# Attention scores made one slot ahead, between the projection part and the value matmuls

## The chip, the cores and the metric

The kernel runs on one NeuronCore of a Trainium2 chip. TensorE (PE; its weight loads are shown as PEld), VectorE (DVE), ScalarE (ACT), GpSimd (POOL) and SyncE (SP) run their own instruction queues, each in order, and meet through semaphores. The metric is the device time of one execution in microseconds (us); the time before is the median of 3 runs, 701.91 us.

## What is computed

One layer, a gated stick-breaking attention, on x of 1024 tokens x 1024 features in float32, with a final RMSNorm:

```python
def stick_breaking_attention(q, k, v):          # 16 heads of 64, blocks of 128 queries
    ...
        mask = key_pos[None, :] < q_pos[:, None]
        z = jnp.einsum('bhqd,bhkd->bhqk', qb, kf) * scale
        log_beta = jax.nn.log_sigmoid(z)
        log_1m = jnp.where(mask, log_beta - z, 0.0)
        after = lax.cumsum(log_1m, axis=3, reverse=True) - log_1m
        a = jnp.where(mask, jnp.exp(log_beta + after), 0.0)
        return jnp.einsum('bhqk,bhkd->bhqd', a, vf)

h = rmsnorm(x, norm_g[0])
q, k, v, gate = jnp.split(h @ w_in, 4, axis=-1)
y = (attention(q, k, v) * silu(gate)) @ w_out
out = rmsnorm(x + y, final_g)
```

The kernel makes a = sigmoid(z) times a running product of sigmoid(-z) from the diagonal down; the running product is one scan on VectorE.

## The kernel before

Heads go in 8 pairs, and each pair has 16 slots; a slot s stands for query block i = s mod 8 of head s // 8 of the pair. Block i has 128 (i + 1) keys, so the work of a block grows through each half of a pair. Pairs 1 to 6 are a loop; pair 7 is written out; after it come the first slots of a tail (pair 8). Every engine runs the same list of slots in its own order, and only semaphores tie them together.

TensorE in slot s (`slot`, L600): the scores of block s (`scores`, L567; slots 0 and 8 make two blocks, slots 1 and 9 none), in slots 6 and 8 a transposition of the values of the next pair (`transpose_v`), 12 matmuls of the next pair's projection (`project_part`, L585; 6 in the first half of pair 7, and parts of the output projection after that), the value matmuls (L632) of the blocks of `a` that were transposed in the slot before, and the transposes (L644) of some blocks of `a`. The transposes of slots 4 to 7 take query blocks 0 to 3 of head 0, slots 8 to 11 blocks 4 to 7 of head 0, slots 12 to 15 blocks 0 to 3 of head 1, and slots 0 to 3 of the next pair blocks 4 to 7 of head 1. So the first transpose of slot 8 and that of the next pair's slot 0 wait (L642, `a_ready`) until the last and widest block, 7 or 15, is finished: "a boundary" in what follows.

ScalarE in slot s: it evacuates a finished projection half on even slots (L719, waits for `proj_done`), in slots 1, 5, 9 and 13 it moves a part of the output sums (L786, waits for the value matmuls of the slot before), then it copies the transposes of slot s-1 out of PSUM (L794; it waits for `t_done`), and only behind these it makes the two sigmoids of block s from the score bank z_ps[s mod 2] (L809 into `rest`, L811 into `a_group`; they wait for `z_ready`). VectorE in slot s: low parts of the splits, the gate product (L982, slots 0 and 14), the low part of the transposed blocks (L1000), and then the scan of block s (L1016). GpSimd in slot s: the product of sigmoid and scan (L1115), which gives `a_ready`, and in s mod 4 = 1 and 2 a weight split behind it (L1091).

The score matmuls wait for `beta_ready` (L576), so a score bank is written again only when the sigmoids of the block two before are done. The transposes and their copies have two banks.

Of the kernel before, what the change touches and what calls it, by code (L numbers as in the profile page):

```python
# [31 lines left out]
SLOTS = 16  # L32
# [41 lines left out]
def is_last(p):  # L74
    return isinstance(p, int) and p == PAIRS - 1


def is_tail(p):
    return isinstance(p, int) and p == PAIRS


def is_first(p):
    return isinstance(p, int) and p == 0


def wait(eng, sem, value):

    if not isinstance(value, int) or value > 0:
        eng.wait_ge(sem, value)
# [16 lines left out]
def v_t_at(p, s):  # L106
    return None if isinstance(p, int) and p >= PAIRS - 1 else STEADY[s][0]


def proj_slots(p):  # L110

    return range(SLOTS // 2) if is_last(p) else range(SLOTS)


def proj_part(p, s):

    if is_last(p):
        return s // 4, 2 * (s % 4), 2 * (s % 4) + 1
    return (s % 4) // 2, 4 * (s % 2), 4 * (s % 2) + 3
# [53 lines left out]
def z_offset(i):  # L173

    return 2 * P if P * (i + 1) == HALF + P else 0


def stick_breaking_layer(nc, x, norm_g, w_in, w_out, final_g, out):
# [3 lines left out]
    with ExitStack() as ctx:  # L182
# [41 lines left out]
        def q_of(par, hh):  # L224
            return arena[:, par, 0, hh * S:(hh + 1) * S]

        def k_of(par, hh, swapped):
            return arena[:, par, 2 if swapped else 1, hh * S:(hh + 1) * S]
# [4 lines left out]
        def w_out_of(half, hl):  # L233
            return arena[:, half, 2 * hl:2 * hl + 2, :].rearrange("p a (b n) -> p (a b) n", n=HALF)
# [70 lines left out]
        block = ctx.enter_context(nc.Block())  # L305
# [176 lines left out]
        def _(pe):  # L482
            def project(ring, bank, half, b):

                for n, (wl, hl) in enumerate(((0, 0), (0, 1), (1, 0))):
                    mm = nc.tensor.matmul(bank[:, :], w_split[:, ring, wl, b, :],  # L486
                                          hT[:, hl, b, half * HALF:(half + 1) * HALF],
                                          start=(b == 0 and n == 0), stop=(b == KB - 1 and n == 2))
                return mm
# [45 lines left out]
            def project_out(n, b):  # L535

                nh, tokens = n // KB, slice((n % KB) * P, (n % KB + 1) * P)
                at = ORDER.index(n)
                partial = n < PARTIAL_TILES and b < PAIRS - 1
                last = PAIRS - 2 if partial else KB - 1  # L540
                first = PAIRS - 1 if n < PARTIAL_TILES and not partial else 0
                if n == 0 and partial or n == ORDER[0] and b == KB - 1 or n == KB:
                    pe.wait_ge(wo_ready, n // KB * KB + b + 1)
                if n in (0, GQ) and b < PAIRS - 1:
                    pe.wait_ge(o_loaded[n // GQ][b], 32)
                if n == ORDER[0] and b == PAIRS - 1:
                    pe.wait_ge(o_lo, 2 * PAIRS)
                if b == first:


                    if n == 0 and partial:
                        pe.wait_ge(stage_ready, 2 * UNITS0 + 8 * (PAIRS - 1) + 2)
                    elif partial or at == 0:
                        pe.wait_ge(partial_sum, n)
                    elif at < BANKS:
                        pe.wait_ge(beta_ready, SLOTS * PAIRS)
                    else:
                        pe.wait_ge(y_sum, at - BANKS + 1)
                bank = proj_ps if partial else y_banks[at % BANKS]
                for m, (ol, wl) in enumerate(((0, 0), (0, 1), (1, 0))):  # L560
                    mm = nc.tensor.matmul(bank[:, :], hT[:, ol, b, tokens], w_out_of(nh, wl)[:, b, :],  # L561
                                          start=(b == first and m == 0), stop=(b == last and m == 2))
                if partial and b == last:
                    mm.then_inc(partial_done, 1)
                return mm

            def scores(p, par, s):  # L567

                hh, i = s // 8, s % 8
                width = P * (i + 1)  # L570
                if s == 0:
                    pe.wait_ge(qk_split, 4 * p + 4)
                    pe.wait_ge(k_swapped, 64 * p + 64)
                    if is_first(p):
                        pe.wait_ge(xt_lo, 2 * KB)
                wait(pe, beta_ready, SLOTS * p + s - 1)  # L576
                z, q, first = z_ps[s % 2], q_of(par, hh)[:, i * P:(i + 1) * P], z_offset(i)
                for c in range(0, first + width, HALF):
                    c0, c1 = max(c, first), min(c + HALF, first + max(width, 2 * P))
                    for swapped in (False, True):  # L580
                        mm = nc.tensor.matmul(z[:, c0:c1], q, k_of(par, hh, swapped)[:, c0 - first:c1 - first],  # L581
                                              start=not swapped, stop=swapped)
                mm.then_inc(z_ready, 1)

            def project_part(p, s):  # L585

                half, b0, b1 = proj_part(p, s)
                unit = 0 if is_last(p) else s // 4
                if half == 0:

                    pe.wait_ge(w_ready, 2 * UNITS0 + 8 * p + 2 * unit + b0 // 4 + 1)
                if b0 == 0:

                    pe.wait_ge(stage_ready, 2 * UNITS0 + 8 * p + 2 * unit + half - (is_first(p) and s == 0))
                for b in range(b0, b1 + 1):
                    mm = project((UNITS0 + unit) % 2, proj_ps, half, b)
                if b1 == KB - 1:
                    mm.then_inc(proj_done, 1)

            def slot(p, par, s):  # L600
                q_late = is_first(p) and s == 0
                if q_late:
                    project_part(p, s)
                if not is_tail(p):

                    for block in {0: (s, s + 1), 1: ()}.get(s % 8, (s,)):
                        scores(p, par, block)
                if v_t_at(p, s) is not None:
                    t = v_t_at(p, s)

                    transpose_v(t_base(p) + t, t % 2, 2 * UNITS0 + 8 * p + 2 + (s == 8), int(s == 8))
                if not is_tail(p) and s in proj_slots(p) and not q_late:
                    project_part(p, s)
                if isinstance(p, int):
                    for _ in range(EARLY_BY_SLOT.get((p, s), 0)):
                        project_out(*early.pop(0))

                for t, av, ahh, grp, j in av_at(p, s):
                    apar = 1 - par if s < 5 else par
                    pe.wait_ge(t_lo, t_base(p) + t + 1)  # L620
                    if j == 0:

                        group = {1: -1, 5: 0, 9: 1, 13: 2}[s]
                        wait(pe, o_summed, 4 * p + group)
                    rel = max(0, j - GQ * grp)
                    for hl in range(2):
                        if rel == GQ - 1:
                            c, moving = HALF - 2 * P, aT_pad[:, hl, :]
                        else:
                            c = rel * P  # L630
                            moving = aT[:, av % 2, hl, c:HALF]
                        mm = nc.tensor.matmul(o_ps[:, c:HALF], v_of(apar)[:, j, 2 * ahh:2 * ahh + 2, :]  # L632
                                              .rearrange("p x d -> p (x d)"), moving,
                                              start=(j == 0 and hl == 0),
                                              stop=(j == GQ * (grp + 1) - 1 and hl == 1))
                    mm.then_inc(av_done, 1)

                for t, av, thh, grp, j in units_at(p, s):
                    wait(pe, t_lo, t_base(p) + t - 1)
                    if j == 0:  # L640

                        pe.wait_ge(a_ready, SLOTS * p + (0 if s < 4 else 4 * (s // 4)))  # L642
                    for i2 in range(max(0, j - GQ * grp), GQ):
                        last = nc.tensor.transpose(t_ps[t % 2][:, i2 * P:(i2 + 1) * P],  # L644
                                                   a_g[grp][:, i2, j * P:(j + 1) * P], ident[:, :])
                    last.then_inc(t_done, 1)

            over_pairs(pe, slot, 4)


# [500 lines left out]
```

## Time and profile before

| | |
|---|---|
| median of 3 runs | 701.91 us (701.83 to 701.91) |
| profiled execution | 702.83 us, span 701.0 us |
| granted TensorE clock, mean | 0.992 |
| PE busy | 673.1 us (96%) |
| PEld busy | 565.2 us (81%) |
| DVE busy | 483.1 us (69%) |
| ACT busy | 426.4 us (61%) |
| POOL busy | 308.0 us (44%) |

A line of a timeline gives the start and the duration in us, the engine, the line of the kernel, the operation, what it writes and reads, how many instructions are merged in it, and in brackets how long its engine was idle ahead of it and what released it. Ends of matmuls are modelled: successive matmuls overlap in the records, so the pace of TensorE is read from the starts.

### The profile page before, as it was taken

Reading aid. Unit: us, or ns where it says so; the run is one execution under the profiler, and the core shown is the slowest. Engines: PE = TensorE matmul, PEld = TensorE weight load, DVE = VectorE, ACT = ScalarE, POOL = GpSimd, SP = SyncE. Lnnn points to the kernel's source line nnn. Section 1 sums busy time; section 2 is a strip of 40 time slices with the busy share of each in tenths; the row PEclk is TensorE's granted clock in tenths of the full one; section 3 lists DMA queues with packets and bytes.
Section 4 is the critical chain, followed back from the end, with each engine's and each line's share of the span. In section 5 each row is a group of like instructions: output and inputs, shape, how many; then the busy total and the mean of one; then the engine's idle time right before and its main releaser. Section 6 shows DMA issues by size and latency. Waiting matters only on the chain.

```text
span 701.0 us, 10872 instructions
## 1 busy us (share of the span) xinstructions
PE 673.1 (96%) x3426; PEld 565.2 (81%) x3426; DVE 483.1 (69%) x636; ACT 426.4 (61%) x795; POOL 308.0 (44%) x225
## 2 busy tenths in 40 slices
PE   5999999999999999999999999999999997999995
PEld 4787888888888888888888888888888776888884
DVE  5835657786678676867677667766776798735565
ACT  5614757676767676767676767666766674622322
POOL 2122544555464546454655464546363643315100
PEclk9999999999999999999999999999999998999998
DMA  7131310141114111510042014201421148522342
GB/s 284 46 95 41 94 43 16 63 119 32 31 57 124 31 32 37 135 39 22 23 135 60 15 31 120 75 15 30 120 60 30 60 136 295 201 91 90 121 146 95
DMA packets 28122, 57.64 MB, mean 82 GB/s; under 512 B 3376, under 2 KB 3376, under 8 KB 28080
## 3 DMA queue, kind: packets, MB, share of 16 engines
q1 hardware_dynamic: 25312, 51.13, 24.2%
q10 hardware_dynamic: 2736, 6.03, 2.3%
q8 instruction: 16, 0.26, 0.1%
q14 instruction: 26, 0.21, 0.1%
q0 software_dynamic: 32, 0.00, 0.0%
HBM read 37.23 MB, written 11.53 MB: 70 GB/s over the span
## 4 chain that ended last, share of the span: by engine, by line
PE 67%; DVE 12%; POOL 10%; issue 7%; ACT 3%; DMA 1%; POOLq 0%; DVEq 0%; ACTq 0%
PE proj_ps L486 31%; PE t_ps L644 8%; PE o_ps L632 8%; PE z_ps L561 8%; DVE rest L1016 7%; PE z_ps L581 5%; POOL a_group L1115 5%; POOL w_split L1091 5%; PE proj_ps L561 4%; PE o_ps L486 2%; DVE aT L1000 1%; DMA a_group<-x 1%; ACT stage L719 1%; ACT gate L776 1%; DVE gate L982 1%
## 5 line engine op out<-in xcount | busy, mean ns | idle before, releaser
L486 PE MATMUL proj_ps<-hT,w_split 128*128 128x512 f32 x1464 | 359.9, 394 | 2.1 <-DVE hT L889 1.4
L486 PEld LDWEIGHTS proj_ps<-hT,w_split 128*128 128x128 f32 x1464 | 269.9, 188 | 57.6 <-DVE hT L889 2.3
L1115 POOL TENSOR_TENSOR a_group<-a_group,rest 128x128 f32<-128x128 f32 (+7 forms) x128 | 160.6, 1257 | 279.2 <-DVE rest L1016 279.2
L1016 DVE TENSOR_TENSOR_SCAN rest<-rest,restart 128x128 f32<-128x128 f32 (+7 forms) x128 | 213.4, 1668 | 16.0 <-ACT rest L809 15.5
L1091 POOL TENSOR_TENSOR w_split<-w_raw,w_split 128x512 fp32r<-128x512 f32 x64 | 115.6, 1807 | 38.0 <-DVE w_split L851 38.0
L1000 DVE TENSOR_TENSOR aT<-t_ps,aT 128x512 fp32r<-128x512 f32 (+2 forms) x160 | 93.2, 607 | 40.1 <-ACT aT L794 38.8
L794 ACT ACTIVATE aT<-t_ps 128x512 fp32r<-128x512 f32 (+2 forms) x160 | 80.2, 532 | 65.8 <-PE t_ps L644 64.6
L581 PE MATMUL z_ps<-arena 128*128 128x512 f32 (+2 forms) x384 | 96.3, 366 | 0.3 <-DVE arena L938 0.3
L938 DVE TENSOR_TENSOR arena<-stage,arena 64x512 fp32r<-64x512 f32 x64 | 43.9, 686 | 69.4 <-ACT arena L739 68.8
L644 PE MATMUL t_ps<-ident,a_group 128*128 128x128 f32 x576 | 84.9, 275 | 4.7 <-POOL a_group L1115 4.4
L809 ACT ACTIVATE rest<-z_ps 128x128 f32<-128x128 f32 (+7 forms) x128 | 83.9, 655 | 8.9 <-PE z_ps L581 8.6
L632 PE MATMUL o_ps<-aT,arena 128*128 128x512 f32 (+2 forms) x320 | 82.9, 365 | 1.7 <-DVE aT L1000 1.7
L811 ACT ACTIVATE a_group<-z_ps 128x128 f32<-128x128 f32 (+7 forms) x128 | 84.3, 659 | 0.0
L644 PEld LDWEIGHTS t_ps<-ident,a_group 128*128 128x128 f32 x576 | 69.4, 142 | 15.1 <-issue 7.1
L719 ACT ACTIVATE stage<-proj_ps 128x512 f32<-128x512 f32 x61 | 36.5, 598 | 62.4 <-PE proj_ps L486 62.4
L632 PEld LDWEIGHTS o_ps<-aT,arena 128*128 128x128 f32 x320 | 60.0, 189 | 16.5 <-DVE aT L1000 3.7
L581 PEld LDWEIGHTS z_ps<-arena 128*128 128x128 f32 x384 | 59.6, 190 | 5.1 <-DVE arena L938 0.8
L561 PE MATMUL z_ps<-arena,hT 128*128 128x512 f32 x246 | 57.7, 391 | 0.0
L786 ACT ACTIVATE oT<-o_ps 64x512 f32<-64x512 f32 x32 | 19.0, 592 | 60.5 <-PE o_ps L632 60.5
L561 PEld LDWEIGHTS z_ps<-arena,hT 128*128 128x128 f32 x246 | 45.8, 188 | 9.4
L990 DVE TENSOR_TENSOR oT<-o_ps,oT 64x512 f32<-64x512 f32 x32 | 22.0, 689 | 24.9 <-ACT oT L786 24.8
L746 ACT ACTIVATE w_split<-w_raw 128x512 fp32r<-128x512 f32 x56 | 35.9, 641 | 0.5
(86 smaller groups left out, 454.2 us busy)
## 6 DMA issues: line engine op xcount, KB each, us to landing
w_raw<-w_in SPq DMA_DIRECT2D x64, 256.0 KB, 2.7
arena<-arena SPq DMA_DIRECT2D x32, 256.0 KB, 4.3
wo_raw<-w_out SPq DMA_DIRECT2D x16, 256.0 KB, 3.7
o_hi_scratch<-o_split SPq DMA_DIRECT2D x14, 256.0 KB, 2.1
o_lo_scratch<-o_split SPq DMA_DIRECT2D x14, 256.0 KB, 2.4
hT<-o_hi_scratch SPq DMA_DIRECT2D x14, 256.0 KB, 4.9
hT<-o_lo_scratch SPq DMA_DIRECT2D x14, 256.0 KB, 5.8
a_group<-x SPq DMA_DIRECT2D x14, 256.0 KB, 3.4
```

The source lines that it names most:

```text
L486: mm = nc.tensor.matmul(bank[:, :], w_split[:, ring, wl, b, :], hT[:, hl, b, half * HALF:(half + 1) * HALF], start=(b == 0 and n == 0), st ...
L561: mm = nc.tensor.matmul(bank[:, :], hT[:, ol, b, tokens], w_out_of(nh, wl)[:, b, :], start=(b == first and m == 0), stop=(b == last and m ...
L581: mm = nc.tensor.matmul(z[:, c0:c1], q, k_of(par, hh, swapped)[:, c0 - first:c1 - first], start=not swapped, stop=swapped)
L632: mm = nc.tensor.matmul(o_ps[:, c:HALF], v_of(apar)[:, j, 2 * ahh:2 * ahh + 2, :] .rearrange("p x d -> p (x d)"), moving, start=(j == 0 an ...
L644: last = nc.tensor.transpose(t_ps[t % 2][:, i2 * P:(i2 + 1) * P], a_g[grp][:, i2, j * P:(j + 1) * P], ident[:, :])
L794: nc.scalar.activation(to, t_ps[t % 2][:, rel * P:HALF], ACT.Copy).then_inc(t_hi, 1)
L809: nc.scalar.activation(rest[:, s % 2, S - width:S], z_ps[s % 2][:, first:first + width], ACT.Sigmoid, scale=-SCALE).then_inc(rest_ready, 1)
L811: nc.scalar.activation(a_g[grp][:, i % GQ, 0:width], z_ps[s % 2][:, first:first + width], ACT.Sigmoid, scale=SCALE).then_inc(beta_ready, 1)
L1000: nc.vector.tensor_tensor(lo, t_ps[t % 2][:, rel * P:HALF], hi.bitcast(F32), ALU.subtract).then_inc(t_lo, 1)
L1016: nc.vector.tensor_tensor_scan(span, span, restart[:, S - 1:(S - 1 - width if width < S else None):-1], 0.0, ALU.mult, ALU.max).then_inc(s ...
L1091: nc.gpsimd.tensor_tensor(to[:, 1], w_raw[:, part, :].rearrange("p (b n) -> p b n", b=4), to[:, 0].bitcast(F32), ALU.subtract).then_inc(w_ ...
L1115: nc.gpsimd.tensor_tensor(a, a, rest[:, s % 2, S + 1 - width:S + 1], ALU.mult).then_inc(a_ready, 1)
```

## The change

In a slot of TensorE the scores move from the front of the slot to behind the projection part (and behind the parts of the output projection), ahead of the value matmuls, and they are those of the next block. The last slot of a pair makes block 0 of the next pair. Each slot of a pair then makes one block of scores. The first slot of the first pair has the order that it had. Nothing is changed on the other engines, and no wait or count is changed.

```diff
             def slot(p, par, s):
-                q_late = is_first(p) and s == 0
-                if q_late:
-                    project_part(p, s)
-                if not is_tail(p):
-
-                    for block in {0: (s, s + 1), 1: ()}.get(s % 8, (s,)):
-                        scores(p, par, block)
                 if v_t_at(p, s) is not None:
                     t = v_t_at(p, s)
 
                     transpose_v(t_base(p) + t, t % 2, 2 * UNITS0 + 8 * p + 2 + (s == 8), int(s == 8))
-                if not is_tail(p) and s in proj_slots(p) and not q_late:
+                if not is_tail(p) and s in proj_slots(p):
                     project_part(p, s)
                 if isinstance(p, int):
                     for _ in range(EARLY_BY_SLOT.get((p, s), 0)):
                         project_out(*early.pop(0))
+
+                if is_first(p) and s == 0:
+                    scores(p, par, s)
+                if s < SLOTS - 1 and not is_tail(p):
+                    scores(p, par, s + 1)
+                elif not is_last(p) and not is_tail(p):
+                    scores(p + 1, 1 - par, 0)
 
                 for t, av, ahh, grp, j in av_at(p, s):
```

## Rows read from the trace of the kernel before

**Rows 1.** Waits, whole span: who waited for whom, us in total, times, longest.
```profile
ACT aT L794 <- PE t_ps L644: 64.6, 61, 3.5
...
ACT rest L809 <- PE z_ps L581: 8.6, 18, 0.7
...
PE t_ps L644 <- POOL a_group L1115: 4.4, 12, 1.2
```
**Rows 2.** Timeline of a steady pair's slots 13 to 15 and next slot 0.
```profile
323.99 0.59 ACT L786 ACTIVATE oT<-o_ps 64x512 f32<-64x512 f32 x1 [1.30 <-PE o_ps L632]
324.14 0.94 PE L581 MATMUL z_ps<-arena 128*128 128x512 f32 x4
...
327.87 1.55 POOL L1115 TENSOR_TENSOR a_group<-a_group,rest 128x768 f32<-128x768 f32 x1 [2.02 <-DVE rest L1016]
...
329.14 0.83 DVE L982 TENSOR_TENSOR gate<-stage,gate 128x512 f32<-128x512 f32 x1 [1.42 <-ACT gate L776]
...
329.37 1.75 POOL L1091 TENSOR_TENSOR w_split<-w_raw,w_split 128x512 fp32r<-128x512 f32 x1
...
330.41 2.59 DVE L1016 TENSOR_TENSOR_SCAN rest<-rest,restart 128x896 f32<-128x896 f32 x1
...
332.51 1.18 PE L581 MATMUL z_ps<-arena 128*128 128x512 f32 x4
332.87 0.38 ACT L794 ACTIVATE aT<-t_ps 128x256 fp32r<-128x256 f32 x1 [1.17 <-PE t_ps L644]
333.15 1.78 POOL L1115 TENSOR_TENSOR a_group<-a_group,rest 128x896 f32<-128x896 f32 x1 [2.03 <-DVE rest L1016]
...
333.53 2.90 PE L486 MATMUL proj_ps<-hT,w_split 128*128 128x512 f32 x12
333.73 1.03 ACT L809 ACTIVATE rest<-z_ps 128x1024 f32<-128x1024 f32 x1 [0.47 <-PE z_ps L581]
...
334.79 2.29 DVE L1016 TENSOR_TENSOR_SCAN rest<-rest,restart 128x1024 f32<-128x1024 f32 x1 [1.07 <-ACT rest L809]
334.88 3.29 POOL L1091 TENSOR_TENSOR w_split<-w_raw,w_split 128x512 fp32r<-128x512 f32 x1
...
336.27 0.40 PE L632 MATMUL o_ps<-aT,arena 128*128 128x256 f32 x2
...
337.85 0.86 DVE L982 TENSOR_TENSOR gate<-stage,gate 128x512 f32<-128x512 f32 x1 [0.77 <-ACT gate L776]
...
338.12 2.45 POOL L1115 TENSOR_TENSOR a_group<-a_group,rest 128x1024 f32<-128x1024 f32 x1
...
340.71 1.06 PE L644 MATMUL t_ps<-ident,a_group 128*128 128x128 f32 x8 [0.34 <-POOL a_group L1115]
```
**Rows 3.** Timeline of a steady pair's slot 7 and slot 8.
```profile
298.10 1.77 POOL L1115 TENSOR_TENSOR a_group<-a_group,rest 128x896 f32<-128x896 f32 x1 [2.02 <-DVE rest L1016]
...
299.23 2.79 DVE L1016 TENSOR_TENSOR_SCAN rest<-rest,restart 128x1024 f32<-128x1024 f32 x1 [0.36 <-ACT rest L809]
...
303.06 2.48 POOL L1115 TENSOR_TENSOR a_group<-a_group,rest 128x1024 f32<-128x1024 f32 x2
```
**Rows 4.** Timeline of the longest stall, in pair 7's slot 8.
```profile
585.26 0.79 PE L632 MATMUL o_ps<-aT_pad,arena 128*128 128x256 f32 x2 [4.16 <-DVE aT_pad L1000]
```
**Rows 5.** Windows (stretch, length, busy of each engine, PEclk, DMA share, GB/s).
```profile
553.70:555.00 1.30, 0.05 (x2) 0.05 (x1) 1.30 (x1) 0.59 (x1) 1.14 (x1) 1.00 0.87 274
585.30:590.00 4.70, 4.70 (x16) 4.22 (x17) 3.77 (x7) 3.37 (x7) 0.84 (x2) 0.50 0.92 285
568.00:586.00 18.00, 12.15 (x61) 9.42 (x61) 17.94 (x16) 11.25 (x20) 10.70 (x6) 0.95 0.54 178
```
**Rows 6.** Timeline of TensorE in a slot 9, which has no scores before.
```profile
306.15 3.02 PE L486 MATMUL proj_ps<-hT,w_split 128*128 128x512 f32 x12
...
309.00 1.10 PE L632 MATMUL o_ps<-aT,arena 128*128 128x512 f32 x4
```
**Rows 7.** Timeline: GpSimd's product of block 15 of pair 7, ahead of the tail.
```profile
614.71 2.00 POOL L1115 TENSOR_TENSOR a_group<-a_group,rest 128x1024 f32<-128x1024 f32 x1 [2.29 <-DVE rest L1016]
```

## The prediction, written before the changed kernel was run

> **What bounds the kernel now.** The busy times come first: TensorE is busy for 673.1 us of a span of 701.0, the others for 483 at most, so what is to be won or lost is in the 28 us in which it isn't, and part of those lies ahead of the first matmul and in the tail. Then the waits, all engines together [rows 1]. There the reader sees three things. ScalarE waits for transposes (L794) 61 times, 64.6 us in all. It waits for scores (L809) only 18 times, 8.6 us. And TensorE itself waits for GpSimd's product (L1115) at the transposes 12 times, 4.4 us. A timeline shows which these are: the boundaries, where the first transpose of slot 8 or slot 0 needs block 7 or 15. There are 15 that the product can end (slot 8 of pairs 0 to 6, slot 0 of pairs 1 to 7, and the tail's slot 0), and TensorE stands at nearly all of them, for 0.2 to 0.35 us in a steady pair. So a steady pair is bound by TensorE, but the chain that ends in `a_ready` arrives at each boundary with no slack. What makes this chain later makes the kernel longer by as much.
>
> The chain at a slot-0 boundary [rows 2]: the transposes of slot 14 leave ScalarE's copy at 332.87; the sigmoid of block 15 starts at 333.73 after 0.47 us of waiting for its scores; the scan starts at 334.79 and ends at 337.08; GpSimd's weight split, 3.29 us long, ends at 338.17; the product of block 15 ends at 340.57; TensorE goes on at 340.71, 0.34 late. One more stall stands by itself, 4.16 us in slot 8 of pair 7 [rows 4], where VectorE is the bound: it is busy for 17.94 of 18.00 us before it [rows 5].
>
> My sums are made against the profiled execution, 702.83 us (span 701.0 and 1.8 around it). The median is 0.92 lower, and I take that off at the end.
>
> **What is the same.** The same matmuls, transposes and waits are issued; no DMA, no instruction of another engine, nothing of SP's queue moves. At the end of a projection part both orders have done the same work, and at the end of slots 0 and 8 as well. So `proj_done` and the boundary's own transposes keep their place if nothing stalls. The scores were made before the projection part of their slot and are now made a slot ahead, so the wait of 0.47 us at L809 goes. I give it nothing: the sigmoid of block s is queued on ScalarE behind the copy of slot s-1's transposes, so early scores lie unused in their bank.
>
> **What becomes late: the transposes.** In slot s the value matmuls and transposes now stand behind the scores of s+1. For the same work done, they end later by the time of these scores. Slot 14: the scores of block 15 start at 332.51 and the projection at 333.53, 1.02 us [rows 2]. The copy at L794 moves from 332.87 to 333.89. It is 0.38 long and the sigmoid can start some 0.26 after its start, at 334.15 in place of 333.73: 0.42 later. Before, the copy lay beside the scores; now it lies behind them. This is the floor of the cost, 0.42 us a boundary.
>
> **It begins two slots earlier and grows in the queues.** In slot 13 the value matmuls are later by the scores of block 13 (0.78: start at 324.14, projection at 324.92), and ScalarE's L786 already waits for them there, 1.30 us [rows 2]. So sigmoid, scan and product of block 13 move by 0.78: the product from 327.87 to 328.65, its end to 330.2. The gate product L982 at 329.1 to 329.4 then meets it. VectorE's operations on two SBUF operands and GpSimd's go one after the other in this trace: the scan at 299.23 takes 2.79 where another of the same shape takes 2.29, and the product of block 6 ends 0.64 after its start [rows 2, 3]; the weight split at 334.88 is 3.29 long, and 1.09 of it is left when the scan ends [rows 2]. By that: L982 runs to 330.8, the weight split to 331.95, the scan of block 14 to 333.85 (before 333.0), the product of block 14 to 335.75 (before 334.93). The scan of block 15 could start at 335.2 but runs from 335.75 to 338.0 (before 337.08), the weight split to 339.1, L982 (0.65) to 339.75 and the product, 2.00 long by itself [rows 7], to 341.75 with a little handing over, where it was 340.57. That is 1.15 us a slot-0 boundary.
>
> The same steps at slot 8 [rows 3]: the product of block 6 ends at about 300.4 (before 299.87), for the scan of block 5 is held back less there; the scan of block 7, before held until 299.87, then ends 0.6 later, and so do the weight split and the product. 0.6 us a slot-8 boundary.
>
> The Trainium skill says of this (SBUF — State Buffer, "Who interferes with whom") that a VectorE operation with two SBUF inputs and a GpSimd operation that reads SBUF hold a common pair of ports in turn, and that whoever issues first blocks the other for the whole instruction. The 3.29 and 2.79 us above agree. By this rule the cost is the 1.15 and 0.6; if the operations only shared bandwidth, it would be the floor, 0.42 at each.
>
> **Last pair.** VectorE is the bound from 568 on, so its lateness counts in full. The copies of slots 3 and 4 are late by the scores of blocks 4 and 5 (0.67 to 0.78), and the backlog begins about 0.65 later. TensorE's clock was 0.50 of full speed after the 4.16 us stall and 1.00 in a stall of 1.25 us in slot 0 [rows 1, 5]. It fell some 3 us into the stall; if it falls and comes back at the same distance from the stall's beginning, 0.65 + 0.3 us less work is done at half speed, which returns 0.45. Net +0.2. Bounds: -5 (stall so short that the clock holds) to +1.5. The tail's boundary: +0.45, for there is no weight split in its chain.
>
> **TensorE's own seams.** A projection part takes 2.74 us from first to next start when it follows scores (333.53 to 336.27 [rows 2]) and 2.85 when it follows transposes (306.15 to 309.00 [rows 6]): 0.11 more. Scores behind transposes carry about 0.09 themselves (1.02 for four matmuls of 512 columns, when twelve take 2.72 or so, 0.227 each: 0.91), which they can lose behind a projection part. Net +0.02 for each of about 105 slots, 2.1 us; bounds 0 and 0.11 x 105 = 11.6.
>
> **The sum.** 7 x 1.15 = 8.05; 7 x 0.6 = 4.2; tail 0.45; pair 7 0.2; seams 2.1: 15.0 us. 702.8 + 15.0 = 717.8, less 0.9 is **716.9 us**.
>
> What is hidden: slot 8's `transpose_v` loses the cover of block 9's scores (0.2 us) against the evacuation it waits for, and slot 0's projection part loses that of block 1's. Both end before the boundary's stall and are absorbed by it. If the stall were gone they would cost 14 x 0.2 = 2.8.
>
> **Rivals.** A difference of 0.2%, 1.4 us, is what can be told from none.
>
> A. Only the direct shift: the queues of VectorE and GpSimd have enough air to take up slots 13 and 14, and just the 0.42 of block 15 is left. 15 x 0.42 = 6.3, seams 0 to 2: 708 to 711 less 0.9, about 708.5. For it: GpSimd is idle for 2.02 us ahead of most products. Against it: in slots 6, 7, 14 and 15 the idle time ends with the scan, which is itself late. Chance 0.25.
>
> B. Faster: the chain to `a_ready` isn't set by the transposes' copy but by the scores; then the 8.6 us of L809 and with them the 4.4 us of TensorE go, from slots 7 and 15 on. The point that decides is whether L809 starts before 333.73 on the steady pair's clock. 702.8 - 4.4 - 0.9 = 697.5. For it: L809 does wait for its scores at each slot 7 and 15. Against it: the copy ahead of it on the same queue waits 1.17 us for transposes, which the change makes late. Chance 0.07.
>
> C. The seams cost the 0.11 in full: 717.8 + 9.5 - 0.9 = 726. Against it: slot 9 as a whole is no longer than its neighbours by that. Chance 0.08.
>
> D. The clock falls in the steady pairs' longer stalls: a stall of 0.34 + 1.15 = 1.5 us is near the 1.25 that it held through, and far from 4.16. If it did, 5.8 us at half speed would cost 2.9 at each slot-0 boundary: +20, 737. Chance 0.03.
>
> E. No difference: the stalls move about and the sum stays within 1.4 us. It needs slack in the chain which 12 stalls say isn't there. Chance 0.05.
>
> The forecast has 0.52. Slower then has 0.52 + 0.25 + 0.08 + 0.03 = 0.88, same 0.05, faster 0.07. The range takes in the forecast with its bounds and rival A: 707 to 723.
>
> **What would show it.** Right: TensorE's wait for L1115 goes from 4.4 us to about 16, with 0.8 at slot 8 and 1.5 at slot 0; L809's wait for scores is gone; L794 starts about 1.0 later in slots 7 and 15 against the projection part; the product of block 14 ends later against it, by 0.8. Wrong: L809 keeps or gains its place (B); stalls of about 0.75 at all boundaries (A); or starts of TensorE that are further apart with no stall (C).

## The result and the profile after

The changed kernel takes 711.65 us (median of 4 runs, 710.38 to 712.5) against 701.87: ratio 1.0133, 95% interval 1.0119 to 1.0147. It is slower by 9.8 us, where 716.9 was forecast with a range of 707 to 723. The profiled execution took 712.5 us (span 710.4), 9.67 more than that of before, and the sums below are made against it.

The page's first part of the kernel after. TensorE is 3.1 us busier than before, VectorE 3.5 us busier, ScalarE 3.0 us less busy, and GpSimd as it was:

```profile
PE 676.2 (95%) x3426; PEld 568.1 (80%) x3426; DVE 486.6 (69%) x636; ACT 423.4 (60%) x795; POOL 308.1 (43%) x225
```

Its waits over the whole span, in the columns of [rows 1]:

```profile
ACT aT L794 <- PE t_ps L644: 90.9, 70, 3.5
...
PE t_ps L644 <- POOL a_group L1115: 7.4, 14, 1.2
...
ACT rest L809 <- PE z_ps L581: 0.7, 1, 0.7
```

The wait of ScalarE for its scores went from 8.6 us to 0.7 [rows 1]. Its wait for the transposes went from 64.6 to 90.9, and TensorE's for the product from 4.4 to 7.4. So the wait moved from the scores to the transposes, which come behind them now.

Where the 9.67 us are is read from the start of the first transpose at each boundary, after less before:

| part | us | forecast |
|---|---|---|
| slot-0 boundaries of pairs 1 to 7, 0.58 to 0.62 each | 4.2 | 8.05 |
| slot-8 boundaries of pairs 0 to 6, 0.16 and six of 0.24 to 0.28 | 1.7 | 4.2 |
| pair 7, slot 0 to slot 8 | 2.0 | 0.2 |
| pair 7, slot 8 to the tail's boundary (the forecast is for that boundary alone) | 1.4 | 0.45 |
| TensorE's seams | no cost of their own | 2.1 |
| behind that | 0.3 | 0 |

Timeline of the kernel after, the boundary that answers to [rows 2] (the same pair; 2.76 us of earlier boundaries lie between the two clocks):

```profile
331.24 1.55 POOL L1115 TENSOR_TENSOR a_group<-a_group,rest 128x768 f32<-128x768 f32 x1 [2.64 <-DVE rest L1016]
...
331.85 1.49 DVE L982 TENSOR_TENSOR gate<-stage,gate 128x512 f32<-128x512 f32 x1 [0.75 <-ACT gate L776]
...
333.73 2.65 DVE L1016 TENSOR_TENSOR_SCAN rest<-rest,restart 128x896 f32<-128x896 f32 x1
...
334.69 1.07 PE L581 MATMUL z_ps<-arena 128*128 128x512 f32 x4
...
335.60 0.53 PE L632 MATMUL o_ps<-aT,arena 128*128 128x384 f32 x2
...
336.10 2.98 PE L486 MATMUL proj_ps<-hT,w_split 128*128 128x512 f32 x12
336.46 0.38 ACT L794 ACTIVATE aT<-t_ps 128x256 fp32r<-128x256 f32 x1 [1.69 <-PE t_ps L644]
336.52 1.77 POOL L1115 TENSOR_TENSOR a_group<-a_group,rest 128x896 f32<-128x896 f32 x1 [2.03 <-DVE rest L1016]
336.74 1.02 ACT L809 ACTIVATE rest<-z_ps 128x1024 f32<-128x1024 f32 x1
...
337.79 2.65 DVE L1016 TENSOR_TENSOR_SCAN rest<-rest,restart 128x1024 f32<-128x1024 f32 x1 [0.49 <-ACT rest L809]
338.25 3.28 POOL L1091 TENSOR_TENSOR w_split<-w_raw,w_split 128x512 fp32r<-128x512 f32 x1
...
341.49 2.44 POOL L1115 TENSOR_TENSOR a_group<-a_group,rest 128x1024 f32<-128x1024 f32 x1
...
344.08 1.07 PE L644 MATMUL t_ps<-ident,a_group 128*128 128x128 f32 x8 [0.83 <-POOL a_group L1115]
```

I count from the last boundary (308.08 here, 305.32 before). The copy L794 starts at 28.38 where it started at 27.55: 0.83 later. The sigmoid has no wait any more and starts 0.25 later (28.66, was 28.41). The product of block 14 is 0.61 later (28.44, was 27.83) and ends at 338.29; the scan of block 15, which its own sigmoid let go 0.24 later, takes 2.65 in place of 2.29 and ends at 32.36 where it ended at 31.76. So 0.25 of the 0.60 comes directly and 0.35 through the wait for GpSimd's product, and the product of block 15 ends 0.60 later. Of these 0.60 TensorE's stall shows 0.49 (0.34 before, 0.83 now). The other 0.1 is what is left of 0.30 more in the slots 15 and 0 (a wait of the projection part for its evacuation above all), less 0.19 that TensorE was ahead when slot 15's projection began. In every second pair that wait is 0.5 us long and the stall 0.42, and the boundary comes no later: what TensorE loses in front of a boundary takes the place of its stall there. So the stalls alone, 7.4 us where they were 4.4, do not show the cost.

In pair 7 TensorE's granted clock fell once more than before. Windows of the kernel after (columns as in [rows 5]), behind the 1.25 us stall of its slot 0:

```profile
562.00:564.50 2.50, 2.50 (x7) 1.92 (x7) 1.89 (x3) 1.24 (x4) 1.40 (x2) 0.50 0.00 0
564.50:566.00 1.50, 1.50 (x7) 1.31 (x6) 0.00 (x0) 0.00 (x0) 0.39 (x1) 0.72 0.00 0
```

A clock of 0.50 for 3.4 us costs about 1.7. Ahead of it there were three waits in a row, of 0.26, 0.56 and 1.25 us; the kernel before has 0.09 and 1.25 there and keeps its clock. And in the output projection a wait for VectorE's partial sum has lost its cover, the work that TensorE did while the sum was made. In the kernel before:

```profile
599.19 2.99 PE L561 MATMUL proj_ps<-arena,hT 128*128 128x512 f32 x12 [0.17 <-DVE stage L1030]
```

In the kernel after:

```profile
607.87 3.02 PE L561 MATMUL proj_ps<-arena,hT 128*128 128x512 f32 x12 [0.77 <-DVE stage L1030]
...
616.44 1.88 PE L561 MATMUL proj_ps<-arena,hT 128*128 128x512 f32 x7 [0.28 <-DVE stage L1030]
```

### The profile page after: what moved, and what is told of

It is laid out like the page before. It is cut to its first block, busy times and chain, and to the rows that moved or that the text cites. A ratio compares the mean times of both kernels' runs of the same rounds, so it can differ in the third digit from the quotient of the medians.

```text
span 710.4 us, 10887 instructions
## 1 busy us (share of the span) xinstructions
PE 676.2 (95%) x3426; PEld 568.1 (80%) x3426; DVE 486.6 (69%) x636; ACT 423.4 (60%) x795; POOL 308.1 (43%) x225
## 4 chain that ended last, share of the span: by engine, by line
PE 64%; DVE 11%; POOL 9%; issue 8%; ACT 6%; DMA 1%; ACTq 0%; POOLq 0%; DVEq 0%
PE proj_ps L486 28%; PE t_ps L644 8%; PE z_ps L561 8%; PE o_ps L632 8%; DVE rest L1016 7%; PE z_ps L581 6%; POOL a_group L1115 5%; POOL w_split L1091 4%; PE proj_ps L561 4%; PE o_ps L486 2%; ACT rest L809 2%; ACT stage L719 1%; PE z_ps L514 1%; DVE gate L982 1%; DVE aT L1000 1%
## 5 line engine op out<-in xcount | busy, mean ns | idle before, releaser
L486 PE MATMUL proj_ps<-hT,w_split 128*128 128x512 f32 x1464 | 368.0, 399 | 3.7 <-ACT stage L719 1.9
L486 PEld LDWEIGHTS proj_ps<-hT,w_split 128*128 128x128 f32 x1464 | 266.2, 189 | 57.8 <-ACT stage L719 3.5
L1016 DVE TENSOR_TENSOR_SCAN rest<-rest,restart 128x128 f32<-128x128 f32 (+7 forms) x128 | 211.1, 1649 | 9.6 <-ACT rest L809 9.1
L794 ACT ACTIVATE aT<-t_ps 128x512 fp32r<-128x512 f32 (+2 forms) x160 | 80.4, 533 | 92.0 <-PE t_ps L644 90.9
L1000 DVE TENSOR_TENSOR aT<-t_ps,aT 128x512 fp32r<-128x512 f32 (+2 forms) x160 | 93.2, 607 | 58.4 <-ACT aT L794 57.3
L581 PE MATMUL z_ps<-arena 128*128 128x512 f32 (+2 forms) x384 | 89.3, 342 | 0.3 <-DVE arena L938 0.3
L809 ACT ACTIVATE rest<-z_ps 128x128 f32<-128x128 f32 (+7 forms) x128 | 83.6, 653 | 0.8 <-PE z_ps L581 0.7
L581 PEld LDWEIGHTS z_ps<-arena 128*128 128x128 f32 x384 | 70.2, 189 | 14.6 <-DVE arena L938 0.8
L632 PEld LDWEIGHTS o_ps<-aT,arena 128*128 128x128 f32 x320 | 57.9, 190 | 10.0 <-DVE aT L1000 2.9
L561 PE MATMUL proj_ps<-arena,hT 128*128 128x512 f32 x138 | 35.7, 407 | 1.1 <-DVE stage L1030 1.0
```

The lines of the kernel that those rows point to most:

```text
L794: nc.scalar.activation(to, t_ps[t % 2][:, rel * P:HALF], ACT.Copy).then_inc(t_hi, 1)
L809: nc.scalar.activation(rest[:, s % 2, S - width:S], z_ps[s % 2][:, first:first + width], ACT.Sigmoid, scale=-SCALE).then_inc(rest_ready, 1)
L1000: nc.vector.tensor_tensor(lo, t_ps[t % 2][:, rel * P:HALF], hi.bitcast(F32), ALU.subtract).then_inc(t_lo, 1)
L1016: nc.vector.tensor_tensor_scan(span, span, restart[:, S - 1:(S - 1 - width if width < S else None):-1], 0.0, ALU.mult, ALU.max).then_inc(s ...
```

## Experiments: which scores cost

`ahead` says in which slots the next block's scores come ahead of the value matmuls; elsewhere they come behind the slot's transposes, the place that they had before.

```diff
-                if s < SLOTS - 1 and not is_tail(p):
-                    scores(p, par, s + 1)
-                elif not is_last(p) and not is_tail(p):
-                    scores(p + 1, 1 - par, 0)
+                ahead = ...      # s % 8 == 0;  s % 8 in (0, 4, 5, 6);  s % 8 not in (4, 5, 6);  s % 8 in (0, 6)
+                if ahead:
+                    next_scores()
                 for t, av, ahh, grp, j in av_at(p, s):
...
                     last.then_inc(t_done, 1)
+                if not ahead:
+                    next_scores()
```

**Blocks 1 and 9 alone.** 

> Only the scores of blocks 1 and 9 are made ahead of the value matmuls (in slots 0 and 8); all others come behind the transposes of the slot before, which is the place that they had. Lateness theory (the change costs because value matmuls and transposes come behind the next block's scores): nothing that the chain to a boundary waits for is later, so 702 us, within 1 of before. Seam theory (TensorE pays where a projection part follows transposes): 14 seams more, at 0.1 us at most, 702 to 703.5; this run cannot tell them apart, it shows that the rest of the change is in the other slots.

Measured: 702.35 us, ratio 1.0002 (0.9993 to 1.0011); no boundary adds or takes more than 0.05 us. But TensorE does lose something, and the boundaries hide it. Its weight loads (PEld) wait for evacuations (at `transpose_v` and the projection part) for 4.8 us in all, 0.9 before, and its waits for the product fall from 4.4 us to 1.6. These are the two waits that the scores of blocks 9 and 1 had covered.

**Blocks 5 to 7.** 

> Blocks 5, 6, 7 of each head (and 1 and 9) are made ahead, the others behind the transposes. Lateness theory: the whole cost of the steady pairs, 0.86 us a pair (0.6 at slot 0, 0.25 at slot 8), is here: slot-0 boundary of pair 7 some 5 to 6 us later than before, and 707 to 710 us in all. Seam theory: cost by the number of moved scores, 3 of 7, so 4 us, 706, and no longer stalls at the boundaries.

Measured: 711.55 us, 1.0130 (1.0114 to 1.0145), the whole cost of the change; the slot-0 boundaries lose 0.62 to 0.65, the slot-8 boundaries 0.25 to 0.31. The estimate of 707 to 710 was too low by what the last pair took: 2.6 us of the 8.7 in its profile come behind slot 0 of pair 7, 1.7 of them with a fall of the clock in its slot 0 as in the changed kernel.

**Blocks 0 to 4.** 

> Blocks 0 to 4 of each head are made ahead, 5 to 7 behind the transposes. Lateness theory: the transposes of slots 4 to 7 and 12 to 15 keep their time, the boundaries' stalls stay at 0.2 to 0.35 us, and what is left is the last pair: 702 to 704. Seam theory: 4 of 7 of the cost, 707.

Measured: 703.46 us, 1.0015 (1.0006 to 1.0024). From pair 0's slot 0 boundary on no steady boundary adds more than 0.03 us or takes more than 0.07, though more scores were moved than in the run above. The waits are nearly those of the run with blocks 1 and 9 (5.3 us for the evacuations, 1.6 for the product), so the blocks moved in addition hide no further cost either. The seam theory falls, and with it rival C. What is left, 1.3 us, is mostly in pair 7: 0.74 of the 0.9 in the profile.

**Block 7 of each head alone.** 

> Only block 7 of each head (and 1 and 9) is made ahead. If the direct shift alone costs (the copy of the transposes behind the widest block's scores, 0.25 to 0.42 us), this is as slow as with blocks 5, 6, 7: 706 to 709. If what began two blocks earlier is handed on through the queues of VectorE and GpSimd, then the slot-0 boundary loses 0.25 in place of 0.6 and the product of block 14 is not late: 704.5 to 706, and some 3 us less than with blocks 5, 6, 7.

Measured: 704.08 us, 1.0030 (1.0018 to 1.0042). A slot-0 boundary loses 0.17, a slot-8 boundary of pairs 1 to 6 nothing (-0.03 to 0.01). The time is 0.4 us under the range that the expectation gave for lateness that is handed on, and its two signs are there: a slot-0 loss of 0.25 or less, and a product of block 14 that is not late. The timeline at the same boundary:

```profile
333.48 1.78 POOL L1123 TENSOR_TENSOR a_group<-a_group,rest 128x896 f32<-128x896 f32 x1 [2.02 <-DVE rest L1024]
...
334.40 1.03 ACT L817 ACTIVATE rest<-z_ps 128x1024 f32<-128x1024 f32 x1
...
335.21 1.29 POOL L1099 TENSOR_TENSOR w_split<-w_raw,w_split 128x512 fp32r<-128x512 f32 x1
335.46 3.19 DVE L1024 TENSOR_TENSOR_SCAN rest<-rest,restart 128x1024 f32<-128x1024 f32 x1 [0.50 <-ACT rest L817]
```

The product of block 14 ends at 335.26, on time, and the scan can start only at 335.46, 0.3 later than before against the last boundary. So the weight split is first now, and the scan stands behind it, 3.19 long. Split and scan together are done 3.39 us after the product of block 14, where they took 3.24 before. So the widest block's own shift (rival A's mechanism) costs 0.17 when it comes alone, and what blocks 5 and 6 add is 0.63 - 0.17 = 0.46 at slot 0, and all of slot 8's 0.27. At slot 8 the product of block 5 already starts 0.26 us late against the last boundary, and everything behind it keeps that distance.

## Experiments: the chain and its cover

**GpSimd's second weight split one slot later**, in the changed kernel and in the kernel before:

```diff
-                if s % 4 in (1, 2) and not is_last(p):
-                    n = 2 * (UNITS0 + 4 * p + s // 4 + 1) + s % 4 - 1
-                    lo_w(n, (UNITS0 + 1 + s // 4) % 2, s % 4 - 1)
+                if s % 4 in (1, 3) and not is_last(p):
+                    n = 2 * (UNITS0 + 4 * p + s // 4 + 1) + s % 4 // 2
+                    lo_w(n, (UNITS0 + 1 + s // 4) % 2, s % 4 // 2)
```

> The changed kernel, and GpSimd makes the second weight split of a group of four slots behind the product of slots 3, 7, 11, 15 in place of 2, 6, 10, 14. Queue theory (the product of block 7 or 15 stands behind a weight split that itself stands behind the scan): the split's 1.1 us go from the chain to each boundary, the stalls of 0.26 and 0.83 us vanish, and 7 x 0.83 + 7 x 0.26, some 6 to 7.5 us of the 9.8 are given back: 704 to 706. If the stalls come from the lateness of the transposes alone and the split lies beside it, nothing changes: 711.7.

> The same move of the second weight split in the kernel before, with scores at the front of the slot. If the chain to the boundaries has no slack there either, its 0.2 to 0.35 us stalls go too: 697.5 to 700. And if the change's cost is only what the chain hands on, this and the changed kernel with the same move differ by the last pair alone, by 3 to 4 us.

Measured: 703.97 us (1.0024, 1.0015 to 1.0033) with the new order, and 697.03 (0.9928, 0.9915 to 0.9942) with the old: 7.7 us and 5.2 us back. TensorE's wait for the product falls from 7.4 to 1.7 us and from 4.4 to 0.4. The weight split ahead of the last product was the link that left the chain without slack, in both orders. Of the 1.7 us that are left in the new order 1.15 stand at pair 7's slot 0; in the old order TensorE waits 1.12 for a low part there instead.

The second expectation was a miss on both counts: 697.03 lies just under its range, and the two differ by 6.9 us, not by 3 to 4. Without the boundary's stall the lost covers show. From one slot 0 to the next the new order takes 71.45 us on average and the old 70.63, 0.82 more. At a slot 0 and around a slot 8 of the new order:

```profile
266.54 3.03 PE L486 MATMUL proj_ps<-hT,w_split 128*128 128x512 f32 x12 [0.54 <-ACT stage L719]
...
372.88 0.60 ACT L719 ACTIVATE stage<-proj_ps 128x512 f32<-128x512 f32 x1 [0.46 <-PE proj_ps L486]
...
373.16 0.27 PE L644 MATMUL t_ps<-ident,a_group 128*128 128x128 f32 x1
373.53 0.42 PEld L495 LDWEIGHTS t_ps<-ident,stage 128*128 128x128 f32 x4 [0.34 <-ACT stage L719]
```

The transposition of the values stands right behind slot 7's transposes and waits 0.34 us for its evacuation; before, the scores of blocks 8 and 9 lay in between. The projection part of slot 0 waits for its evacuation in the same way, for 0.10 to 0.54 us in each steady pair. And in four of the six steady pairs the projection part of slot 1 comes 0.47 us late, behind the weight split that now follows the product of block 15. No cover is lost there, for both orders have made the same scores by then; it is the chain that is late. In the pair of [rows 2] this product starts 3.47 us before that projection part could start, where it starts 3.93 before it with the old order, and takes 2.53 in place of 2.00.

**Scores used early**: in the changed kernel, ScalarE makes L809 ahead of the copies L794 (and, in the first of two kernels, VectorE the scan ahead of the low parts L1000).

```diff
...
+                    act.wait_ge(z_ready, SLOTS * p + s + 1)
+                    wait(act, a_ready, SLOTS * p + s - 1)
+                    nc.scalar.activation(rest[:, s % 2, S - width:S], ..., ACT.Sigmoid, scale=-SCALE).then_inc(rest_ready, 1)
                 for t, av, _, ugrp, j in (units_at(p, s - 1) if s else av_at(p, 0)):
...
-                act.wait_ge(z_ready, SLOTS * p + s + 1)
-                wait(act, a_ready, SLOTS * p + s - 1)
-                nc.scalar.activation(rest[:, s % 2, S - width:S], ..., ACT.Sigmoid, scale=-SCALE).then_inc(rest_ready, 1)
```

> The changed kernel, and ScalarE makes the sigmoid that the scan needs ahead of the copies of the transposes, and VectorE the scan ahead of the low part of the transposed blocks. So the early scores are used early. Queue theory: the scan of block 15 starts when ScalarE and the port are free, 1 to 1.5 us earlier against the projection part; the boundary stalls of 0.26 and 0.83 us vanish and at least 6 of the 9.8 us come back, 700 to 706; the last pair, where VectorE is the bound, may go either way by 3 us. If the copy behind the scores is not what makes the chain late, it stays at 710 to 712. If the low parts then come too late for the value matmuls, which have 3.1 us from the transposes, it is slower than 712.

> The changed kernel, and ScalarE alone makes the sigmoid for the scan ahead of the copies of the transposes; VectorE keeps its order, low parts and then the scan. In slots 14 and 15 ScalarE was idle for 0.3 and 1.7 us ahead of the copies, and the sigmoid partly fits in there, so the scan of block 15 may start some 0.3 us earlier: 708 to 711. If the copies are late by the sigmoid in every slot, the value matmuls wait for the low parts as they did when the scan went first too, and it is slower than 712.

Measured: 731.7 us (1.0420, 1.0406 to 1.0434) with both, 716.32 (1.0195, 1.0181 to 1.0209) with ScalarE's alone. Both are the bad branch of their expectation. TensorE's waits in the first:

```profile
PE o_ps L632 <- DVE aT L1009: 23.2, 26, 2.5
...
PE o_ps L632 <- DVE aT_pad L1009: 3.0, 4, 1.4
```

The boundary stalls are gone, and the value matmuls wait for the low parts instead, 26 times. In the second the slot-0 boundaries lose 1.15 to 1.19 us: the copies are late by a part of the sigmoid, the low part and the scan stand behind them in order, and the product is later still. In this kernel the scores can't overtake the transposes' copy without loss: it feeds the value matmuls of the same slot.

**The long stall of pair 7.** VectorE makes the gate product L982 behind the low part and ahead of the scan (in all slots, old order; the expectation says behind the scan too, which the edit doesn't do):

```diff
-                if gate_at(p, s):
-                    ...
                 for t, av, _, grp, j in (units_at(p, s - 1) if s else av_at(p, 0)):
...
+                if gate_at(p, s):
+                    ...
                 if is_tail(p):
                     return
```

> The kernel before, and VectorE makes the gate product of a slot behind the low parts and the scan, not ahead of them. This is for the one long stall, 4.16 us in slot 8 of pair 7, and the clock behind it. The low part that TensorE waits for comes 2.5 us earlier, the stall is 1.7 us; if the clock at 0.5 for 6.8 us is due to the stall, it stays at 1.0 and 2.9 us more are won: 696 to 698. If the clock falls by itself: 699.5.

Measured: 701.21 us, 0.9989 (0.9980 to 0.9999), a miss in size. Timeline of the stall:

```profile
582.98 0.50 PE L632 MATMUL o_ps<-aT_pad,arena 128*128 128x256 f32 x2 [1.78 <-DVE aT_pad L993]
...
584.73 1.06 PE L644 MATMUL t_ps<-ident,a_group 128*128 128x128 f32 x8 [1.25 <-POOL a_group L1115]
```

The 4.16 us fell to 1.78, and in the profiled execution the clock stayed at 1.00 until the very end of the kernel, where it had been 0.50 for 6.8 us behind the long stall. So that fall went with the stall, but not in a fixed measure: the two kernels below have waits of 1.76 and 1.24, and of 1.74 and 1.25, at this place, and there the clock was 0.50 for 3.4 us. And the product is late there as well, 1.25 us (a branch that the expectation does not name), and six of the seven slot-0 boundaries up to pair 7's lost 0.16 to 0.20 each, while one gained 0.34.

**Both edits that helped**, the gate product moved in slot 8 of pair 7 only, on the old order and on the new:

> The kernel before with both edits that helped: the second weight split behind the product of slots 3, 7, 11, 15, and the gate product behind the low part in slot 8 of pair 7 only. If the gains add, 697.0 less the 2.9 us that the later gate product took from the last pair: 694 to 695. If the boundary of slot 8 of pair 7 then waits for its product (1.25 us) as much as it waited for the low part, 696.

> The changed kernel with the same two edits: 704.0 less 2 to 3, 701 to 702. The order of the scores then costs what is left without the stalls at the boundaries: 6 to 7 us if it is seams and covers, as the two kernels with the late split alone differ by (704.0 and 697.0).

Measured: 696.47 us (0.9921, 0.9907 to 0.9935) on the old order, the second branch of its expectation, and 702.67 (1.0007, 0.9998 to 1.0016) on the new, 0.7 above the expected range. The first is the fastest kernel of this study, but not by more than its uncertainty against the late split alone. The scores' order costs 6.2 us still.

**Pair 7 in the old order.** The changed kernel with `ahead = not is_last(p) or s % 8 == 0`.

> The changed kernel, but in pair 7 blocks 2 to 7 and 10 to 15 have their scores behind the transposes again. The boundaries up to slot 0 of pair 7 stay 5.9 us late; what slots 0 to 8 of pair 7 added (2.0) falls to 0.5 if it is VectorE's lateness there, and stays if it is the clock that fell in slot 0; the 1.4 of its second half goes, for the output projection has its cover against the partial sum back. 708.5 to 710.

Measured: 708.85 us, 1.0096 (1.0080 to 1.0111), so 2.8 us of the 9.8 are pair 7. Up to its slot 0 nearly all is as after (5.69 us late in the profile, 5.95 there); slots 0 to 8 then add nothing in place of 2.04, and the second half 0.18 in place of 1.36. The same 1.24 us stall stands in its slot 0 and the clock does not fall behind it:

```profile
561.00:563.00 2.00, 2.00 (x14) 1.73 (x13) 1.56 (x3) 1.64 (x4) 1.66 (x2) 1.00 0.00 1
563.00:566.00 3.00, 3.00 (x19) 2.59 (x18) 1.70 (x4) 1.46 (x3) 0.64 (x1) 1.00 0.00 0
```

So the 1.24 us stall alone does not bring the fall. The other profiles add to this. Behind the same stall of 1.24 or 1.25 us the clock fell for 3.4 us in the changed kernel, in the one with blocks 5 to 7 ahead and in the one with ScalarE's sigmoid first, where the wait just before the stall was 0.56, 0.56 and 1.07 us; it held in this one (0.50), and in the kernel before and those with blocks 1 and 9, 0 to 4 and 7 ahead (0.09 or less). Each is one execution, so this is a pattern and not a proof. Of the four executions of the changed kernel two had a mean clock of 0.989 and two of 0.991; 3.4 us at half speed make 0.0024. With blocks 5 to 7 ahead, slots 0 to 8 of pair 7 add 1.75 us with the same fall. By that some 1.7 of the 2.04 are the clock and 0.3 the early scores of the narrow blocks, where VectorE is the bound; the division was not measured by itself.

## Why the prediction was right

**The direction and the mechanism held.** "Early scores lie unused in their bank", and the transposes behind them are late: the copy moved by 0.83 and L809's wait went. That blocks 5 to 7 carry all of the steady pairs' loss, and blocks 0 to 4, on the same queues but far from a boundary, none of it, is shown by the two kernels that split them. The sizes did not hold: 9.7 us were measured in the profile and 15.0 forecast, and TensorE's wait for the product, which was to go to about 16 us, is 7.4.

**The direct shift, 0.42 us, was mis-sized; it measured 0.25.** The copy came 0.83 later and not 1.02, because TensorE was 0.19 ahead when slot 15's projection began: from the boundary to there the new order takes 28.02 us and the old 28.21. The forecast took the scores' 1.02 us from the row behind transposes, and behind a projection part the same four matmuls take 0.91 (334.69 to 335.60). That is the same error as the seam term, 2.1 us: a projection part does take 2.82 now where it took 2.74, but the scores lose as much or more. The forecast's own figures say so. It put what the scores can lose at 0.09, while its 1.02 less its 0.91 is 0.11, as much as the projection part was to gain.

**The queues' share was right in kind and too large.** At slot 0 1.15 was forecast and 0.60 measured; at slot 8 0.6 and 0.25. Some 0.2 of the difference at slot 0 is the start: the product of block 14 was put 0.8 late and was 0.61, for the scores moved in front of slot 13's value matmuls took 0.69 us and not 0.78 (326.02 to 326.70 on the new clock), and TensorE was 0.1 ahead there. Another 0.1 is the scan, which ended 2.15 us behind that product and not 2.25. And 0.25 is a wrong sum of the forecast: behind the weight split it counted 0.65 for L982 and 2.00 for the product, 2.65, when [rows 2] have 2.40 from the end of the split (338.17) to that of the product (340.57). After the change it is 2.40 again. The turns themselves held: the scan of block 15 was held until 338.29, when the product of block 14 ended, and took 2.65 us. In the kernel with block 7 alone the order is turned: the split starts first and takes 1.29 us, where the shortest of that trace takes 1.28, and the scan takes 3.19. The Trainium skill says (SBUF — State Buffer, "Who interferes with whom") that whoever issues first keeps the other out for the whole instruction. The traces agree, with 2.65 and 3.19 against 2.29; if the two only shared bandwidth, the split that started first should have been longer than its shortest too. The result that the forecast drew from it, a cost over the direct shift, was found (0.35 of 0.60).

**Pair 7 was missed: 0.65 us forecast with the tail's boundary, 3.4 measured.** Two things failed. The clock was put as falling only behind the long stall; it fell in slot 1 too, behind 1.25 us and two shorter waits, which the forecast had held to be safe since the same 1.25 had been safe before (rival D, in one place and for 3.4 us). And the wait for the partial sum was overlooked: the scores of blocks 12 and 14 had covered it, 0.17 before, 0.77 and 0.28 after. So the total is better than its terms. The steady pairs were 6.3 us too dear and the seams 2.1, pair 7 was 2.8 too cheap, and that this made up for a third of it, leaving 5.3 us in the profile, is luck.

**What was hidden and named came out.** The forecast named 2.8 us for `transpose_v` and slot 0's projection part "if the stall were gone". The kernel with blocks 1 and 9 alone shows these waits while the stall still takes them up, and the new order with a late split shows them in the time: 0.82 a pair together with the split's wait, 5.7 over seven.

Rival A (0.42 direct, no queues, 708.5) lay nearer to the time, 3.2 us off against the forecast's 5.3, than its mechanism deserves: block 7 alone costs 0.17 at a slot-0 boundary and nothing at slot 8. Rivals B, D at each boundary, and E fell: each of the 14 boundaries came later, and the 0.83 us stalls left the clock at 1.00.

## What to carry to other kernels

Work that is made earlier pays only if the engine that consumes it can reach it; here the consumer's queue had a copy in front of it, and the early work pushed exactly that copy's source back. Letting the consumer take the early work first lost more still, for the copy had a deadline of its own. Before moving a block, list what it is moved ahead of, what it covered, and how much slack the next deadline has: at slot 8 a lateness of 0.26 us that the product of block 5 already had was paid in full, two blocks later. A stall can also hide what a change costs, and the cost comes out when the stall is mended. And look for the link that took the slack: moving one weight split out of the chain won 5 us where reordering the scores lost 10.

## What was not expected of the hardware

- In these traces four float32r matmuls of 512 columns take 1.02 us from start to next start behind transposes and 0.91 behind a projection part; twelve take 2.74 behind scores and 2.82 to 2.85 behind transposes. The extra goes with coming behind transposes, whichever group it is.
- TensorE's clock held at 1.00 through stalls of 1.25 and 1.78 us and fell behind one of 4.16; behind a stall of 1.24 or 1.25 us in slot 0 of pair 7 it fell for 3.4 us in three profiled executions and held in five, and the three had the longest waits just before that stall (0.56 and more).
- A VectorE scan and a GpSimd weight split on SBUF operands change places when the scan comes 0.3 us later, and the pair is done in about the same time either way (3.24 and 3.39 us behind the product ahead of them; the instructions are 3.28 and 2.65 long in one order, 1.29 and 3.19 in the other).
